# The last 512-column matmul of each down product, split into two of 256 columns

## The reference, cut to what matters

```python
D_MODEL = 1024; SEQ = 256; D_FF = 2816

def swiglu(x, w_gate, w_up, w_down):
    return (jax.nn.silu(x @ w_gate) * (x @ w_up)) @ w_down

# first block
x = layer_norm(alpha * x + 0.5 * swiglu(x, w_gate[0], w_up[0], w_down[0]), ln_g[0], ln_b[0])
x = layer_norm(alpha * x + hybrid_mixer(x, ...), ln_g[1], ln_b[1])
x = layer_norm(alpha * x + 0.5 * swiglu(x, w_gate[1], w_up[1], w_down[1]), ln_g[2], ln_b[2])
...
# second block
f = rmsnorm(h, norm_ffn_pre) @ w_up
f = causal_dwconv(f, conv_ffn) + conv_ffn_b
f_gate, f_val = jnp.split(f, 2, axis=-1)
f = (jax.nn.gelu(f_gate) * f_val) @ w_down
h = h + rmsnorm(f, norm_ffn_post)
```

## Time and profile before

| | us |
|---|---|
| median of 3 runs | 1179.62 |
| lowest and highest | 1177.43, 1182.71 |
| the profiled execution | 1177.42 |
| its span, first to last instruction | 1175.6 |

### The profile page before, as it was taken

One profiled execution on the slowest core, in us unless ns is written; L12 is line 12 of the kernel. 1 busy time (PEld: TensorE's weight loads), 2 busy tenths in 40 slices (PEclk: granted clock), 3 DMA queues, 4 the chain that ended last, 5 costly groups with the idle time before them and its releaser, 6 DMA issues.

```text
span 1175.6 us, 22455 instructions
## 1 busy us (share of the span) xinstructions
PE 1107.0 (94%) x8040; PEld 1029.5 (88%) x8040; DVE 519.4 (44%) x939; ACT 626.5 (53%) x1004; POOL 910.3 (77%) x700
## 2 busy tenths in 40 slices
PE   6999998999999998999999799899999988999985
PEld 6999997998898897999998789899899787999974
DVE  3423115402335565723112546775565344465654
ACT  5444445555556765444444765554556565554563
POOL 7899996998552596999998599483435778999973
PEclk9999999999998999999999899999999999999998
DMA  7866664576431455666666376243223554665641
GB/s 246 323 205 199 195 193 149 160 201 200 121 109 54 126 165 157 191 203 200 195 197 198 92 210 193 93 147 90 73 91 110 182 184 146 188 191 191 196 148 69
DMA packets 52631, 193.40 MB, mean 165 GB/s; under 512 B 5840, under 2 KB 6096, under 8 KB 51920
## 3 DMA queue, kind: packets, MB, share of 16 engines
q1 hardware_dynamic: 50976, 184.57, 51.7%
q10 hardware_dynamic: 1584, 7.81, 1.8%
HBM read 191.31 MB, written 1.05 MB: 164 GB/s over the span
## 4 chain that ended last, share of the span: by engine, by line
POOL 52%; issue 31%; PE 15%; DVE 2%; POOLq 1%; ACT 0%; DVEq 0%; ACTq 0%
POOL weights_low L499 52%; PE banks L530 8%; PE acc L530 6%; POOLq L502 0%; DVE xs L1883 0%; DVE stat L1898 0%; DVE res L1910 0%; DVE res L1896 0%; POOLq L496 0%; DVE xs L1916 0%; DVE acc L1880 0%; DVE act_buf L1759 0%; ACT tmp L1466 0%; DVE hf L1767 0%; POOLq L499 0%
## 5 line engine op out<-in xcount | busy, mean ns | idle before, releaser
L499 POOL TENSOR_TENSOR weights_low<-ring,weights_high 128x512 fp32r<-128x512 f32 x696 | 910.1, 1340 | 246.6 <-ACT weights_high L1226 243.6
L1226 ACT CAST weights_high<-ring 128x1024 fp32r<-128x1024 f32 x348 | 361.6, 1048 | 235.2 <-PE banks L530 108.8
L530 PE MATMUL banks<-xT_high,weights_high 128*128 128x256 f32 x1488 | 417.6, 281 | 2.7 <-POOL weights_low L499 2.5
L530 PE MATMUL banks<-xT_low,weights_high 128*128 128x256 f32 x1488 | 413.4, 278 | 0.0
L530 PE MATMUL banks<-xT_high,weights_low 128*128 128x256 f32 x1488 | 413.1, 278 | 0.0
L530 PEld LDWEIGHTS banks<-xT_high,weights_high 128*128 128x128 f32 x1488 | 280.7, 189 | 8.2 <-issue 2.3
L530 PEld LDWEIGHTS banks<-xT_low,weights_high 128*128 128x128 f32 x1488 | 280.6, 189 | 2.2
L530 PEld LDWEIGHTS banks<-xT_high,weights_low 128*128 128x128 f32 x1488 | 280.2, 188 | 0.0
L1734 DVE TENSOR_TENSOR hf<-act_buf,banks 128x256 f32<-128x256 f32 x40 | 16.8, 421 | 223.5 <-ACT act_buf L1252 223.5
L530 PE MATMUL acc<-weights_high,hT_high 128*128 128x512 f32 x264 | 103.7, 393 | 4.0 <-POOL weights_low L499 3.6
L530 PE MATMUL acc<-weights_low,hT_high 128*128 128x512 f32 x264 | 104.2, 395 | 0.0
(11 more groups left out here) (345 smaller groups left out, 1602.3 us busy)
## 6 DMA issues: line engine op xcount, KB each, us to landing
ring<-in_stream SPq DMA_DIRECT2D x348, 512.0 KB, 4.0
rows<-in_big_rows ACTq DMA_DIRECT2D x3, 1024.0 KB, 5.8
rows<-in_big_rows ACTq DMA_DIRECT2D x3, 512.0 KB, 4.1
cst<-in_consts ACTq DMA_DIRECT2D x1, 1411.0 KB, 12.8
gates<-in_x_fm SPq DMA_DIRECT2D x2, 512.0 KB, 5.6
xs<-in_x_tm ACTq DMA_DIRECT2D x1, 1024.0 KB, 8.9
out<-xs SPq DMA_DIRECT2D x4, 256.0 KB, 2.1
p_in<-in_p_fm ACTq DMA_DIRECT2D x1, 256.0 KB, 2.8
```

The costliest lines, as they stand in the source:

```text
L499: last = nc.gpsimd.tensor_tensor(wlo[:, slot, hs], ring[:, slot, hs], whi[:, slot, hs].bitcast(F32), ALU.subtract)
L530: ins = nc.tensor.matmul(o, lhsT, rhs, start=start, stop=stop, **kw)
L1226: nc.scalar.copy(whi[:, ch % RING, :], ring[:, ch % RING, :]).then_inc(S["hi_ready"], 1)
```

## The change

The three matmuls of each `mm3` in `down` are written out. For the last of the four products of a down product (`half` 1, `tok` 1) the third matmul, 128x128 of `hT_low` times 512 columns of `weights_high`, is made as two matmuls with the same stationary operand, over columns 0 to 255 and 256 to 511 of the same bank. `down_done` is raised by the second.

```diff
                     for half in range(2):
                         w = loop_weights(4, it)
                         for tok in range(2):
-                            ins = mm3(acc[:, 2 * tok + half, :], cut(hT, f % GROUP, slice(P * tok, P * tok + P)), w, very_first, False,
-                                      skip_group_check=True)
+                            o, x = acc[:, 2 * tok + half, :], cut(hT, f % GROUP, slice(P * tok, P * tok + P))
+                            tm_high(o, x, w, very_first, skip_group_check=True)
+                            parts_of = ((0, 2 * T),) if (half, tok) != (1, 1) else ((0, T), (T, 2 * T))
+                            for lo, hi in parts_of:
+                                ins = mm(o[:, lo:hi], x[1], w[0][:, lo:hi], False, False, skip_group_check=True)
                     ins.then_inc(S["down_done"], 1)
```

## The result

The changed kernel took 1191.06 us (median of 5 runs, 1189.78 to 1193.08), the kernel before 1179.11 (5 runs, 1177.43 to 1182.71). The ratio is 1.0086, with an interval of 1.0061 to 1.0112. The forecast of 1179.5 was wrong, and the time lies just above its range, which ended at 1190.5. The direction and the mechanism are those of the first rival, which had 0.29.

What follows compares the result with a forecast made beforehand. TensorE was taken to bound the feed-forward stages. The split's -0.002 us a round, -0.1 us over 57, took the median from 1179.62 to 1179.5 us, with a range of 1176.8 to 1190.5.

Steps and rivals of the forecast that it cites:

- the first rival: Gate and up product behind the split stays at the slow 0.1178 us per matmul: +9.6 us over 51 rounds, chance 0.29.
- What bounds the kernel: Feed-forward stages: TensorE sets the pace, 8.22 us a round, so each ns per round reaches the end 57 times.
- The pair is covered: Two 256-column halves in the down product: added weight load hidden, -0.002 to +0.007 us a round; uncovered had chance 0.03.
- The semaphores and VectorE: End of the down product: slot-free semaphore comes at the same time to 0.01 us, and VectorE, waiting for ScalarE, isn't late.
- I take the entry of rows 5 as it is, begun two matmuls earlier: Step into 256-column matmuls: same five gaps of 0.593 us, then the quick 0.1133; round from 8.213 to 8.211 us.
- 51 equal events: Evidence against the slow rate: in three feed-forward stages, all 51 entries behind a 512-column stream came out quick.
- an unlike one: Further evidence against the slow rate: the entry at 500.18 us, four gaps long instead of five, also came out quick.
- the two matmuls fewer: Possible cause of the slow rate: the 256-column stream is entered after 11 matmuls of 512 columns, before after 12.
- the wait on the first load: Possible cause of the slow rate: the gate and up product's first load, waiting on a semaphore, now falls into the entry.
- 48 x 0.1178 - 5.466 = 0.188 us: Cost per round if the gate and up product's 48 matmuls run slow: 5.654 us in place of 5.466.
- no difference: Whole kernel: forecast with its small variants (entry shorter, one stage slow), range 1176.8 to 1182.5 us, chance 0.64.
- Two ends of the range: Median time: 1176.8 us from the full -1.6 and -1 for spread; 1190.5 from 1189.2 and 1 for spread.

## Why the prediction was wrong

- **What bounds the kernel: right.** TensorE alone sets the pace of the feed-forward stages, and what a round loses arrives at the end: 12.2 us by the rounds, 11.95 by the medians.
- **The pair is covered: right.** Its halves take 0.113 to 0.120 us in every kernel, and with all twelve split a quick down product takes 2.72 us where the twelve of 512 took 2.75. The semaphores and VectorE were right too.
- **"I take the entry of rows 5 as it is, begun two matmuls earlier": this step failed.** It assumed that the entry depends on nothing but that a 512-column stream is left. All entries behind 512 columns in the trace of before were quick, but nearly all of them also left the cycle of three gaps at one and the same place, twelve being a multiple of three. I counted 51 equal events as 51 witnesses (and one of them, at 500.18 us, a second time as an unlike one). The split leaves the cycle one gap earlier, behind 229, and a half on weights that stands there is slow (the changed kernel, the kernels with the wait, the increment and the order moved, and the ninth split). Behind 232 it is quick at once, behind 226 slow. In place of 5.466 us the 48 matmuls then took 5.651. The cycle stands in the starts of the trace of before; I saw only its mean in the rows.
- **It takes the place and the pair.** With the first of the twelve split, eleven matmuls of 512 columns stand directly ahead of the gate and up product, one short of a full cycle as in the changed kernel, and it is quick. What is slow behind 229 is a 256-column matmul that still streams weights, and the step from there into `xT` keeps the slow rate.
- **The rival's mechanism: right; its cause half right; its size too small.** I gave as causes the two matmuls fewer and the wait on the first load. The wait is out (with it moved, all stays slow). The term 48 x 0.1178 - 5.466 = 0.188 us was right to 0.003 (measured 5.651 - 5.466 = 0.185). What it lacked is that a slow gate and up product hands the slow rate to the 512-column matmuls behind it, at 0.2333 us each, +0.05 us a round. With 0.240 for 51 rounds the rival comes to 12.2 us, which on the median of before in these five runs (1179.11) makes 1191.4; it was 1191.06.
- **Why it doesn't heal.** With the pair at the end, a round that starts slow leaves the 512-column cycle (233, 233, 234) slow and stays slow over the step, 48 times out of 48; the rounds hand it on. Without the pair it does heal: where a slow 512-column stream ran directly into the gate and up product, that product came out quick (four of four without the last matmul, and the one with the first split, from 971.95 us). That is why a difference of a few ns at one place becomes 1%: it chooses which of two self-repeating rounds runs.
- **The chances.** 0.64 for no difference and 0.29 for the rival came from the count of entries. With two rates in the trace that both last once entered, and a change that shifts the entry, the row of quick entries supports only the entry as it was. Two ends of the range were also added up loosely (1189.2 + 1 is 1190.2, 1179.5 - 1.6 - 1 is 1176.9); the measured time lies outside either way.
- **Left open.** Why a change of the moving operand from weights to `xT` turns a quick stream, why a slow one turns or not by its length (of those with 24 halves ahead of `xT`, with all split, nearly all turn; of those with 25, nearly none), why the step from 512 columns directly into `xT` goes with 236 or with 229 behind equal gaps, and what in the chip the cycle of three is, no run here tells. The rules are what was seen, no mechanism of the hardware.

## What to carry to other kernels

Where an engine runs without a gap and the trace shows one shape at two rates, ask which rate each stretch has and what sets it at its start, before costing an edit by durations; many equal rounds are one observation of it. An edit that looks free in columns and instructions can choose the other rate for all that follows, so compare a few places for it: here the same split cost 1% on the last matmul and nothing that can be measured on the first.

## What the runs showed of the hardware

- Streams of float32r matmuls of 256 columns, each with its own load, ran at 0.1133 or 0.1178 us each at the full granted clock. Over 280 on end kept either rate, in two executions of one and the same program. The Trainium skill, TensorE: Matmul & The Clock Gate, section Back-to-back issue gap, gives N / 2.4 + 2.5 for what it calls the isolated gap at the full clock; for 256 columns that makes an estimate of 109.2 ns. No stream of 24 or more here went below 113.3.
- 512-column ones ran at 0.229 (as 226, 229, 232) or at 0.2333, the second behind a slow 256-column stream.
- Where the width changed on one moving operand, the rate went with the place in the cycle of three gaps (439 of 439 cases in the table above, those behind a slow stream included). Where a quick 256-column stream changed from the weights to `xT`, it turned slow (181 of 182). Moving the semaphore wait (1192.91 us), the increment (1190.76 us) or the operands' high and low parts (1191.12 us) left the slow rounds as they were, and one more matmul into a foreign PSUM bank, on weights, turned no quick stream (four cases).
